# Experts' rows through slots in memory, gate times up formed ahead of a low half, a shorter router chain, and squares added by Pool

## The reference

```
logits = tok @ router_w + router_b;  probs = softmax(logits)
top_p, top_i = top_k(probs, 2);  gate = one_hot(top_i) * top_p / sum(top_p)
for ex in range(8):
    y = y + gate[:, ex] * ((silu(g) * up) @ w_down[ex])     # g, up = tok @ w_gate_up[ex], 3584 wide each
```

## Time and profile before

| | us |
|---|---|
| median of 3 timed runs | 1633.96 (1633.31 to 1634.13) |
| the profiled execution | 1633.86 |
| its span, first to last instruction | 1631.3 |
| busy: PE, DVE, ACT, POOL | 1524.7, 1207.1, 1045.7, 30.8 |
| stretch of the eight experts' steps | 601 to 1616 |

### The profile page before, as it was taken

How to read it: one execution, slowest core, us unless ns; L and a number is a source line. 1 busy time by engine, 2 the same in 40 slices (tenths; PEclk the granted TensorE clock), 3 DMA queues, 4 the chain that set the end, 5 groups by cost and what they waited for, 6 DMA issues and landing times.

```text
span 1631.3 us, 22094 instructions
## 1 busy us (share of the span) xinstructions
PE 1524.7 (93%) x8110; PEld 1299.9 (80%) x8110; DVE 1207.1 (74%) x1203; ACT 1045.7 (64%) x1109; POOL 30.8 (2%) x48
## 2 busy tenths in 40 slices
PE   7787999997788859999999999999999999999996
PEld 6787999997676857887887887887887887887884
DVE  6675545436645358978988988988888988888896
ACT  6874444443655246776767776777767777777775
POOL 2000000000200110000000000000000000000000
PEclk9998999998899869999999999999999999999998
DMA  8345455541312229999999999999999999999993
GB/s 262 120 129 165 155 181 169 170 143 56 107 52 78 65 79 340 361 330 355 358 331 358 356 345 342 351 350 347 341 358 343 348 355 340 344 360 341 343 364 126
DMA packets 222352, 424.87 MB, mean 260 GB/s; under 512 B 7760, under 2 KB 76624, under 8 KB 222304
## 3 DMA queue, kind: packets, MB, share of 16 engines
q1 hardware_dynamic: 222128, 423.68, 74.8%
q0 software_dynamic: 176, 0.53, 0.1%
HBM read 423.13 MB, written 1.05 MB: 260 GB/s over the span
## 4 chain that ended last, share of the span: by engine, by line
PE 83%; DVE 8%; ACT 5%; issue 3%; DMA 0%; ACTq 0%; DVEq 0%; SPq 0%
PE bank L401 25%; PE bank L402 24%; PE bank L403 24%; DVE w_lo L1563 2%; PE bank L670 2%; ACT w_hi L1189 2%; PE bank L705 1%; PE bank L422 1%; DVE w_lo L1303 1%; PE bank L651 1%; DVE x_lo L1651 1%; ACT w_hi L939 1%; DVE mix_sq L1317 1%; DVE rstd L1312 1%; PE bank L442 1%
## 5 line engine op out<-in xcount | busy, mean ns | idle before, releaser
L1563 DVE TENSOR_TENSOR w_lo<-raw,w_hi 128x2048 fp32r<-128x2048 f32 x338 | 768.2, 2288 | 143.3 <-ACT w_hi L1189 139.9
L1189 ACT CAST w_hi<-raw 128x2048 fp32r<-128x2048 f32 x338 | 645.4, 1916 | 268.6 <-PE bank L403 268.6
L401 PE MATMUL bank<-w_hi,x_hi 128*128 128x512 f32 x896 | 367.6, 410 | 5.6 <-DVE x_lo L1651 4.8
L403 PE MATMUL bank<-w_hi,x_lo 128*128 128x512 f32 x896 | 350.6, 391 | 0.0
L402 PE MATMUL bank<-w_lo,x_hi 128*128 128x512 f32 x896 | 350.5, 391 | 0.0
L1303 DVE TENSOR_TENSOR w_lo<-raw,w_hi 128x2048 fp32r<-128x2048 f32 (+8 forms) x93 | 153.0, 1668 | 168.2 <-ACT w_hi L939 168.1
L401 PEld LDWEIGHTS bank<-w_hi,x_hi 128*128 128x128 f32 x896 | 168.8, 188 | 50.7 <-issue 12.7
L401 PE MATMUL bank<-u_hi,w_hi 128*128 128x272 f32 (+2 forms) x632 | 188.0, 298 | 19.0 <-DVE u_lo L1331 8.7
L402 PEld LDWEIGHTS bank<-w_lo,x_hi 128*128 128x128 f32 x896 | 168.9, 188 | 40.5 <-issue 7.7
L403 PEld LDWEIGHTS bank<-w_hi,x_lo 128*128 128x128 f32 x896 | 168.6, 188 | 36.4
L402 PE MATMUL bank<-u_lo,w_hi 128*128 128x272 f32 (+2 forms) x632 | 185.8, 294 | 0.0
(11 more groups left out here) (274 smaller groups left out, 1642.2 us busy)
## 6 DMA issues: line engine op xcount, KB each, us to landing
raw<-in_m_w_gate_up SPq DMA_DIRECT2D x226, 1024.0 KB, 7.1
raw<-in_m_w_down SPq DMA_DIRECT2D x112, 1024.0 KB, 7.2
raw<-in_f_w_gate_up SPq DMA_DIRECT2D x24, 1024.0 KB, 5.1
raw<-in_f_w_down SPq DMA_DIRECT2D x12, 1024.0 KB, 5.1
raw<-in_a_w_in SPq DMA_DIRECT2D x10, 1024.0 KB, 7.4
raw<-in_a_w_out SPq DMA_DIRECT2D x8, 640.0 KB, 4.3
raw<-in_b_w_o SPq DMA_DIRECT2D x4, 1024.0 KB, 5.2
raw<-in_b_w_uq SPq DMA_DIRECT2D x4, 576.0 KB, 4.1
```

Of the source, the lines that this page charges most:

```text
L401: nc.tensor.matmul(o, a[0], b[0], start=start, stop=False)
L403: return nc.tensor.matmul(o, a[1], b[0], start=False, stop=stop)
L1189: nc.scalar.copy(w_hi[(NC0 + c) % SPLIT][:], raw[slot][:]).then_inc(hi_done, 1)
L1563: nc.vector.tensor_tensor(w_lo[s][:], raw[(NC0 + c) % RAW][:], w_hi[s][:].bitcast(F32), ALU.subtract)\
```

## The change

The experts' rows go through two arrays in device memory, `x_slots` and `y_slots`, of (16 + 1) x 128 rows each. Pool fills both with zeros during attention (34 stores of 0.5 MB), and ScalarE waits for that before it empties `b_out`'s tiles, whose squares lie where the zeros came from. After the router, Pool scatters the normed tokens `u_tok` to `x_slots` by index; each step loads its 128 rows from there (`x_rows`) and stores the last expert's `y_exp`, unscaled, to `y_slots`. In the last step Pool gathers each token's two rows, scales and adds them; expert 7's rows alone still go through a matmul with `selT` after the loop. For expert 0, x is made by float matmuls of `u_tok` with `sel`, already turned.

In a step the gate and up parts are taken in pairs of tiles (eight chunks, the last tile alone four), and the chunks are cut otherwise: 2 blocks of k by 1024 columns for 4 by 512, and down weights as four neighbouring rows for each partition, so that a partition's run in memory is 4 and 8 KB where it was 2 and 4. `e_h` is turned by columns four apart to fit. VectorE forms gate times up before the low half that follows it in order. Gates come from the difference of the two top logits in place of a softmax. The sum of squares of all but the last tile of a post-norm is formed by Pool (`add_squares`), and TensorE sums one array for them. At the end the table load and the product with the gain stand ahead of the root.

```diff
+            def sum_added(name, at=ALL):
+
+                pe.wait_ge(sq_added, ADDED[name])
+                nc.tensor.matmul(banks[6 + NORM[name] % 2][:, at], ones, sq[:, 0, at], start=True, stop=False)
...
-                if m:
-                    sum_emptied("ao", "a_out", m - 1, sq[:, m - 1, :])
+            sum_added("ao")
...
-                if q:
-                    for m in (2 * q - 2, 2 * q - 1):
-                        sum_emptied("fo", "f_down", m, sq[:, m, :])
-            for m in (KD - 2, KD - 1):
-                sum_emptied("fo", "f_down", m, sq[:, m, :])
+            sum_added("fo")
+            sum_emptied("fo", "f_down", KD - 1, sq[:, KD - 1, :])
...
-            def token_squares(k):
-
-                pe.wait_ge(sq_ready, SQ["m"] + k + 1)
-                for b, (t0, n) in enumerate(TB):
-                    last = nc.tensor.matmul(banks[6][0:n, NB * NE + b:NB * NE + b + 1], sq[:, k, t0:t0 + n],
-                                            ones[:, 0:1], start=False, stop=False)
-                return last
...
             for k in range(KD):
                 pe.wait_ge(res_done, RES["bo"] + k + 1)
                 for b, (t0, n) in enumerate(TB):
-                    nc.tensor.matmul(banks[6][0:n, NE * b:NE * b + NE], hT[:, k, t0:t0 + n], gw[:, k, :],
-                                     start=False, stop=False)
-                for b, (t0, n) in enumerate(TB):
-                    last = nc.tensor.transpose(banks[2 * b + k // 4][0:n, P * (k % 4):P * (k % 4) + P],
+                    last = nc.tensor.transpose(banks[2 * b + k // 4][:, P * (k % 4):P * (k % 4) + P],
                                                hT[:, k, t0:t0 + n], ident)
                     if k % 4 == 3:
                         mark(last, ("h_tok", b, k // 4))
-                if k:
-                    token_squares(k - 1)
-            token_squares(KD - 1)
-            last = nc.tensor.matmul(banks[6][:, 0:NB * NE + NB], ones, zeros, start=False, stop=True)
+                for b, (t0, n) in enumerate(TB):
+                    nc.tensor.matmul(banks[6][:, NE * b:NE * b + NE], hT[:, k, t0:t0 + n], gw[:, k, :],
+                                     start=False, stop=False)
+            last = nc.tensor.matmul(banks[6][:, 0:NB * NE], ones, zeros, start=False, stop=True)
...
-            def gather(half):
-
-
-                for part, src in enumerate((h_thi, h_tlo)):
-                    for b in range(NB):
-                        last = nc.tensor.matmul(banks[half][:, :], sel[:, b, :], src[:, b, NT * half:NT * half + NT],
-                                                start=(part == 0 and b == 0), stop=(part == 1 and b == NB - 1))
-                return last
...
+                    last = nc.tensor.matmul(banks[2 + k // 4][:, P * (k % 4):P * (k % 4) + P],
+                                            u_tok[:, b, P * k:P * k + P], sel[:, b, :], start=(b == 0), stop=(b == NB - 1))
+                if k % 4 == 3:
...
+                def turn(u):
+
+                    js = up_tiles(u)
+                    pe.wait_ge(eh_done, it * UT + (js[-1] + 1))
+                    if u:
+                        pe.wait_ge(eh_lo_done, it * UT + js[0])
+                    for j in js:
+                        for f in range(4):
+                            last = nc.tensor.transpose(banks[6 + j % 2][:, P * f:P * f + P],
+                                                       e_h[:, j % 2, bass.ds(f, P, step=4)], ident)
+                    emark(last, ("turned", u))
+
...
-                            if c in SCATTER:
-
-                                i = SCATTER.index(c)
-                                if i == 0:
-                                    pe.wait_ge(selT_done, it + 1)
-                                    pe.wait_ge(y_done, it * 2 + 2)
-                                if i >= 3:
-                                    pe.wait_ge(added, it * 4 + (i - 1))
-                                emark(scatter(banks[(7, 4, 5)[i % 3]], i % NB, i // NB), ("scattered", i))
-                    if j:
-                        turn(j - 1)
+                for c in range(4 * UT):
+                    wc = echunk(c)
+                    bank_ready(c)
+                    u, g, k0, kn, w_cols = up_part(c)
+                    for i, bank in enumerate(UP_BANKS[u][g]):
+                        for k in range(kn):
+                            last = product(banks[bank][:, :], (x_hi[:, k0 + k, :], x_lo[:, k0 + k, :]),
+                                           [x[:, k, NT * i:NT * i + NT] for x in wc], k0 + k == 0, k0 + k == KD - 1)
+                    emark(last, ("chunk", c))
+                    if c in TURNS:
+                        turn(TURNS.index(c))
...
-                    if d == 1:
-
-                        for b in range(NB):
-                            last = nc.tensor.matmul(banks[7][:, 0:1], sel[:, b, :].bitcast(F32), cur[:, 3 + b:4 + b],
-                                                    start=(b == 0), stop=(b == NB - 1))
-                        emark(last, ("gate",))
-                        for b in range(NB):
-                            last = nc.tensor.transpose(banks[2][:, P * b:P * b + P], sel[:, b, :].bitcast(F32), ident)
-                        emark(last, ("selT",))
-                    if d == 3:
-                        turn(UT - 1)
-
-                    if d == 5:
-                        pe.wait_ge(sel_done, it + 2)
-                        slot_norms()
-                    if d in (5, 6):
-                        emark(gather(d - 5), ("xs", d - 5))
+                    bank_ready(4 * UT + d)
+                    if d == 6:
+                        pe.wait_ge(x_landed, it * 16 + 16)
                     if d in (8, 9):
-                        pe.wait_ge(xs_done, it * 2 + (d - 8 + 3))
                         last = turn_x(d - 8)
                         if d == 9:
...
-                dn = w["m_w_down"][0, bass.ds(e, 1)].rearrange("a (k p) n -> p (a k) n", p=P)
+                dn = w["m_w_down"][0, bass.ds(e, 1)].rearrange("a (j p i) n -> p (a j) (i n)", p=P, i=4)
                 for c in range(chunks):
                     slot = (NC0 + c) % RAW
+                    if c == 8:
+                        sp.wait_ge(y_done, it * 2 + 2)
+                        sp.dma_start(y_slots[bass.ds(it * P, P), :], y_exp[:]).then_inc(y_stored, 16)
+                    if c == 16:
+                        sp.wait_ge(x_hi_done, it + 1)
+                        sp.wait_ge(x_sent, 16 * 2 * NB)
+                        sp.dma_start(x_rows[:], x_slots[bass.ds(it * P + P, P), :]).then_inc(x_landed, 16)
 
                     sp.wait_ge(lo_done, it * EC + (NC0 + c - RAW + 1))
                     if c < 4 * UT:
-                        j, g, kh = c // 4, c // 2 % 2, c % 2
-                        src = up[:, 4 * kh:4 * kh + 4, EF * g + NT * j:EF * g + NT * j + NT]
+                        u, g, k0, kn, w_cols = up_part(c)
+                        src = up[:, k0:k0 + kn, EF * g + 2 * NT * u:EF * g + 2 * NT * u + w_cols]
                     else:
-                        f = 2 * (c - 4 * UT)
-                        src = dn[:, f:f + 2, :]
+                        d = c - 4 * UT
...
+            def add_squares(name, tile, at=ALL):
+
+                for m in range(1, KD - 1):
+                    pool.wait_ge(emptied["A"], EMPTIED[TN[(tile, m)]])
+                    if m > 1:
+                        pool.wait_ge(sq_added, ADDED[name] - (KD - 1 - m))
+                    nc.gpsimd.tensor_tensor(sq[:, 0, at], sq[:, 0, at], sq[:, m, at], ALU.add).then_inc(sq_added, 1)
+
+            add_squares("ao", "a_out")
+            add_squares("fo", "f_down")
...
+            pool.wait_ge(krope_copied, 3)
+            at(pool, "sum", "cq")
+            nc.gpsimd.memset(blank, 0.0).then_inc(blank_done, 1)
+            pool.wait_ge(blank_done, 1)
+            for i in range(2 * NE + 1):
+                pool.dma_start(x_slots[P * i:P * i + P, :], blank).then_inc(zeroed, 16)
+                pool.dma_start(y_slots[P * i:P * i + P, :], blank).then_inc(zeroed, 16)
+
+            add_squares("bo", "b_out", REAL)
             pool.wait_ge(res_done, RES["bo"] + 1)
...
+            pool.wait_ge(zeroed, ZEROED)
+            pool.wait_ge(u_done, 2 * NB)
+            pool.wait_ge(index_done, 1)
+            for k in range(2):
+                for b in range(NB):
+                    i = NB * k + b
+                    pool.indirect_dma_start(x_slots[:], picks(x_index[:, i:i + 1]), u_tok[:, b, :], None)\
+                        .then_inc(x_sent, 16)
...
+            pool.wait_ge(y_stored, rounds * (NE * 16))
+            nc.gpsimd.tensor_tensor(gate[:, NB:2 * NB], gate[:, 0:NB], gap, ALU.mult).then_inc(acc_done, 1)
+            for i in range(2 * NB):
+                pool.indirect_dma_start(picked[:, i, :], None, y_slots[:], picks(y_index[:, i:i + 1]))\
+                    .then_inc(y_picked, 16)
+            pool.wait_ge(y_picked, 16 * 2 * NB)
...
```

(63 more changed lines are left out.)

418 lines of the change are left out of this document (203 added, 215 removed).

## The result

The changed kernel takes 1585.6 us (median of 4 runs, 1584.5 to 1586.6) beside 1634.1 for the kernel before (4 runs): ratio 0.9703, 95% interval 0.9691 to 0.9716. The forecast was 1563, so 48.5 us were gained of 70.5. The profiled execution took 1584.7 (span 1582.9).

A forecast was written before the change was run, and what follows sets the result against it. TensorE was taken to pace the kernel, not the DMAs. Loop 50.4, post-norms 6.8, router 13.3 and tail 2.0, less 2.0 in the last step, gave 70.5 us: 1563 us, bounds 1553 to 1578, 8 in 10 for 1553 to 1604.

The forecast's parts named there:

- rival B: Loop: turns of e_h, read four elements apart, are paced slower; doubled 1582 us, fourfold 1620; chance 0.11.
- rival A: Loop: the DMAs are full, w_hi waits for landed chunks; 1639 us at 348 GB/s, 1590 at 365; chance 0.14.
- Loop: Experts' steps: 6.3 us of work leaves TensorE, period 126.5 to 120.2; eight steps give 50.4 us.
- Last step: Last expert step: Pool's gather, scalings and adds can hold VectorE; 2 us lost (0 to 6).
- Post-norms and router: Squares leave TensorE at the post-norms (6.8 us); shorter chain from router to first expert product (13.3 us).
- b_out's end: End of the b_out post-norm: about one sum of squares leaves TensorE, 0.4 us, counted with the router.
- Tail: Kernel's end: table load moves to where ScalarE waits, two operations move ahead of the root; about 2 us saved.
- C: Before b_out: Pool's zero fills end late; one behind another 1572 us, at 4 us each 1616; chance 0.07.

The follow-up runs named there:

- before_off96: The kernel before with 96 bytes of unused space behind `cur`, moving eh_hi, eh_lo, x_hi and x_lo as the change did; 1652.1 us (ratio 1.0109).
- all_aligned: The changed kernel with 160 bytes a partition before eh_hi, putting all four stationary operands a multiple of 256 bytes from the weight buffers; 1568.5 us (0.9604).
- pace_map: Separate kernel of only 3072 products of 128x512, other engines idle, operand addresses moved against each other; 0.2267 us a product at 0, 0.2342 at 96.
- turns_near: The changed kernel with e_h turned by neighbouring columns and down weights loaded in 4 KB runs in place of 8 KB; 1581.7 us (0.9672).
- norms_on_tensor: The changed kernel without Pool's adds, the three post-norms' squares summed by TensorE tile by tile as before; 1595.8 us (0.9761).
- x_aligned: The changed kernel with 32 bytes unused behind `first`, so eh_hi, eh_lo, x_hi and x_lo start at multiples of 128 bytes; 1582.5 us (0.9685).

## Why the prediction was partly right

The mechanism was right: the removed work left TensorE, which still paces, and nothing else became late but for a moment in the last step. One term was mis-sized, the loop's. The measured time lies above the forecast's own range (1553 to 1578) and inside the wider one (1553 to 1604). It lies between rival B's 1582 and rival A's 1590 by coincidence, since neither of the two is what happened.

**Loop, 50.4 forecast, 26.1 had.** The step that failed is "Nothing takes their place on TensorE: the 504 weight products stay". They stay in number, not in pace. 504 x (0.2342 - 0.2280) = 3.1 us a step went there, of the 6.3 that were to be gained. The cause is shown three ways: the move of 96 bytes alone slows the kernel before (before_off96), undoing it gives the changed one 17.1 us (all_aligned), and TensorE alone shows the same numbers (pace_map). The Trainium skill, TensorE: Matmul & The Clock Gate, Step-by-step: what each phase is for, says that loading the next tile's weights takes no read bandwidth in SBUF from the running matmul. By that the distance should not matter; pace_map shows 0.2267 to 0.2342 by it, and the measurement decides. Whether it is the loading of the stationary tile that disturbs the moving one was not shown: no run changed the number of loads.

A second, smaller miss is the turns: "28 turns ... keep their number and are only grouped otherwise". TensorE after, and for comparison before:

```profile
728.28 1.24 PE L698 MATMUL bank<-con,e_h 128*128 128x128 f32 x8
729.27 0.48 PE L428 MATMUL bank<-w_hi,x_hi 128*128 128x512 f32 x1
```

```profile
752.98 0.60 PE L705 MATMUL bank<-con,e_h 128*128 128x128 f32 x4
753.33 0.48 PE L401 MATMUL bank<-w_hi,x_hi 128*128 128x512 f32 x1
```

Eight take 0.99 and four took 0.35, so three groups of eight and one of four (0.39) cost 3.35 where seven of four cost 2.45: 0.9 us a step, of which turns_near shows 0.13 x 3 to be the stride. What the sum then lacks, about 1 us a step in the changed kernel's favour, stands in TensorE's timeline. The forecast had "The short wait at a step's boundary, where x_lo stands between two low halves, stays". It shrank, the kernel before first and then the changed one:

```profile
979.08 0.50 PE L401 MATMUL bank<-w_hi,eh_hi 128*128 128x512 f32 x1 [0.51 <-DVE w_lo L1563]
```

```profile
823.20 0.50 PE L428 MATMUL bank<-w_hi,eh_hi 128*128 128x512 f32 x1 [0.17 <-DVE w_lo L1593]
```

With the products next to it, this place took 1.17 us a step more than the pace before and 0.45 after: 0.7. before_off96 shows that the slower pace alone takes 0.5 of that, as VectorE gets more time. Besides, the first product behind a group of turns takes 0.09 longer than the others (729.27 to 729.59 is 0.32), and there are six such groups a step where there were ten.

**Last step, -2.0 forecast, -2.3 had.** The mechanism was there. Pool, then VectorE, then TensorE:

```profile
1487.43 7.12 POOL L959 TENSOR_TENSOR acc<-picked 128x1024 f32<-128x1024 f32 x2
```

```profile
1488.18 4.15 DVE L1593 TENSOR_TENSOR w_lo<-raw,w_hi 128x2048 fp32r<-128x2048 f32 x1 [0.27 <-ACT w_hi L1228]
```

```profile
1493.58 1.23 PE L698 MATMUL bank<-con,e_h 128*128 128x128 f32 x8 [2.25 <-DVE e_h L1703]
```

A low half of 2.3 us takes 4.15 while Pool adds, and TensorE waits 2.25 us for the `e_h` behind it. Those 1.9 us more are most of the wait. The low half also began late, released by a high half that had waited for its chunk:

```profile
1486.22 1.92 ACT L1228 CAST w_hi<-raw 128x2048 fp32r<-128x2048 f32 x1 [0.64 <-DMA raw<-in_m_w_gate_up]
```

From 1455 to 1490, with Pool's gather, its scaling and the weights under way, the DMAs moved 409 to 415 GB/s at a share of 1.02 to 1.03. What those late loads cost by themselves was not tried.

**Post-norms and router, 20.1 forecast, 21.4 had.** The reciprocal behind b_out's sum came 8.3 us earlier (7.2 forecast with b_out's end); by norms_on_tensor 7.5 of that are Pool's adds. The rest fits the 272-column products, which ran at 0.1253 us after and in before_off96, and at 0.1260 before: a gift of the move that no term held. From there to the first product 13.1 us were saved (12.9 forecast; the router's own terms ahead of its reciprocal add to 5.3 where 5.0 was written). Pool's adds fell between a_out's tiles and held nobody up: no row of TensorE waits for Pool. In the loop's first 4 us the kernel before had half the clock (10 products between 600.94 and 605.00), the changed one the whole: about 2 us that no term of mine held:

```profile
600.94:605.00 4.06, 4.06 (x10) 3.21 (x11) 1.95 (x1) 0.00 (x0) 0.00 (x0) 0.51 0.19 30
```

**Tail, 2.0 forecast, 2.1 had**: from the last scatter to the end 13.1 us, where 15.2 were.

From the first product to the last scatter the loop took 990.3 us for 1015.2, 24.9 less: 26.1 - 2.3 + 2.0 for the clock, less 0.9 that I can't place. With the other two, 24.9 + 21.4 + 2.1 = 48.4.

**Rivals.** A, the DMAs full: no wait of `w_hi` for a load between 700 and 1400, 367 GB/s in the window and 377 in all_aligned's; the pace of 0.234 is the same in stretches of 3 us from 197 to 426 GB/s. Only in the last step did its sign appear (6.0 us of ScalarE's waits, above). B: a fifth of its lower price. C: each fill took 17 us to land, for 2.7 of the row it was priced by, but they overlapped: ScalarE emptied b_out's first tile at 526.30, released by TensorE and not by a DMA.

```profile
x_slots<-mix_sq POOLq DMA_DIRECT2D x17, 512.0 KB, 17.0
y_slots<-mix_sq POOLq DMA_DIRECT2D x17, 512.0 KB, 17.9
```

```profile
526.30 0.39 ACT L990 ACTIVATE mix_sq<-bank 128x256 f32<-128x256 f32 x1 [1.92 <-PE bank L430]
```

## What to carry to other kernels

A change that allocates anything ahead of the matmuls' operands moves them, and 96 bytes cost 17 us of 1600 here: after every change compare the distance from start to start of an untouched product before looking for waits. Where stationary and moving fp32r tiles stream through 128x512 products, keep their distance a multiple of 256 bytes. Count on less than the faster products promise: 3.5 us a step were worth 2.4 here, as TensorE then waits for what it used to find ready. A term "these instructions stay" holds for their count; their duration is a number to be checked in the new trace.

## What the runs showed of the hardware

The pace of 128x512 fp32r products of two operands in SBUF depends on their distance modulo 256 bytes: 0.2267 us at 0, 0.2290 at 192, 0.2325 at 128, 0.2332 to 0.2342 elsewhere (steps of 32 bytes were tried, no finer ones). It needs no other engine: in pace_map the others were idle and the DMA share was 0.01 at most. What inside TensorE or the memory makes it is not shown.

The 272-column products moved the other way and by less: 0.1260 us before and in x_aligned, 0.1253 after, in before_off96 and in all_aligned (means of over 1600 products with `u_hi` in each). Their moving tiles lie 1088 bytes apart, so the distance takes all multiples of 64 in turn in the first two, and 32 more than these in the other three. They were not measured by themselves, so the rule of 256 bytes is shown for 128x512 products alone.
